# Short-conv rows behind the last input slab, fewer products per LayerNorm statistic, and two swish buffers

## The reference

```python
z = h @ w_in                                   # 7 groups of 1024 columns
b_a, c_a, x_a, u_b, v_b, g_a, g_b = jnp.split(z, cuts, axis=-1)
y_a = (b_a * depthwise_conv(c_a * x_a, conv_a)) @ w_a_out      # 3 taps
u = u_b * jax.nn.sigmoid(v_b)
u = depthwise_conv(u, conv_b) + b_conv_b                       # 31 taps
u = jax.nn.silu(layernorm(u, ln_g, ln_b))                      # over the 1024 channels
y_b = u @ w_b_out
m = jax.nn.sigmoid(g_a) * y_a + jax.nn.sigmoid(g_b) * y_b
return m @ w_o
```

## Time and profile before

| | |
|---|---|
| time, median of 3 runs | 1763.46 us (1763.32 to 1764.2) |
| the profiled execution's own time | 1762.71 us |
| its span, first to last instruction | 1760.9 us |
| mean granted TensorE clock | 0.961 of full speed |
| busy: PE, VectorE (DVE), ACT, GpSimd (POOL) | 1587.8, 1336.4, 682.0, 339.0 us |

### The profile page before, as it was taken

One profiled execution on the slowest core, in us unless ns is written; L12 is line 12 of the kernel. 1 busy time (PEld: TensorE's weight loads), 2 busy tenths in 40 slices (PEclk: granted clock), 3 DMA queues, 4 the chain that ended last, 5 costly groups with the idle time before them and its releaser, 6 DMA issues.

```text
span 1760.9 us, 21630 instructions
## 1 busy us (share of the span) xinstructions
PE 1587.8 (90%) x7040; PEld 1290.2 (73%) x7040; DVE 1336.4 (76%) x1152; ACT 682.0 (39%) x574; POOL 339.0 (19%) x208
## 2 busy tenths in 40 slices
PE   2799999999999997997989965999999999999981
PEld 2688888888888885775777854788887777777861
DVE  5687869678696878349435446999999999899984
ACT  4401121121111202214213122777776766676762
POOL 1100000000000000000000002255454444345440
PEclk9999999999999998998999975999999999999995
DMA  7413323142232315423426253999999999999945
GB/s 267 142 54 115 107 94 108 60 131 83 84 107 95 107 48 194 128 72 120 132 85 201 101 203 124 348 366 371 373 360 361 361 351 358 359 352 356 370 143 208
DMA packets 167572, 352.07 MB, mean 200 GB/s; under 512 B 17229, under 2 KB 90957, under 8 KB 167542
## 3 DMA queue, kind: packets, MB, share of 16 engines
q1 hardware_dynamic: 150838, 309.71, 49.9%
q0 software_dynamic: 16704, 41.98, 7.9%
HBM read 323.84 MB, written 46.66 MB: 210 GB/s over the span
## 4 chain that ended last, share of the span: by engine, by line
PE 59%; DMA 18%; DVE 13%; issue 4%; ACT 4%; POOL 1%; DVEq 0%; SPq 0%; POOLq 0%; ACTq 0%
PE ps L1220 18%; PE ps L1222 18%; PE ps L1221 18%; DMA e_raw<-in_w_down_dram 15%; DVE e_lo L1148 3%; ACT e_hi L723 2%; DMA xg<-d_h,g_idx 2%; DVE e_lo L1144 2%; PE ps L1276 2%; DVE macc L836 1%; PE ps L1394 1%; PE ps L1342 1%; DVE s L951 1%; DVE conf L942 1%; DVE f_o L1210 1%
## 5 line engine op out<-in xcount | busy, mean ns | idle before, releaser
L1220 PE MATMUL ps<-A_hi,w_hi 128*128 128x512 f32 x1024 | 402.9, 393 | 23.8 <-DVE A_lo L931 13.0
L1221 PE MATMUL ps<-A_lo,w_hi 128*128 128x512 f32 x1024 | 401.0, 392 | 0.0
L1222 PE MATMUL ps<-A_hi,w_lo 128*128 128x512 f32 x1024 | 400.9, 392 | 0.0
L1144 DVE TENSOR_TENSOR e_lo<-e_raw,e_hi 128x2048 fp32r<-128x2048 f32 x136 | 309.0, 2285 | 12.4 <-ACT e_hi L717 10.8
L921 DVE SCALAR_TENSOR_TENSOR conv_acc_b<-glu,colc,conv_acc_b 128x1024 f32<-128x1024 f32 x232 | 298.0, 1285 | 10.4 <-DVE rows L913 0.3
L717 ACT CAST e_hi<-e_raw 128x2048 fp32r<-128x2048 f32 x136 | 259.7, 1912 | 61.3 <-PE ps L1222 56.1
L1220 PEld LDWEIGHTS ps<-A_hi,w_hi 128*128 128x128 f32 x1024 | 194.0, 189 | 66.9 <-issue 17.8
L1221 PEld LDWEIGHTS ps<-A_lo,w_hi 128*128 128x128 f32 x1024 | 194.1, 190 | 40.7 <-issue 0.5
L1222 PEld LDWEIGHTS ps<-A_hi,w_lo 128*128 128x128 f32 x1024 | 193.8, 189 | 40.6
L1220 PE MATMUL ps<-e_hi,xT_hi 128*128 128x512 f32 x528 | 212.6, 403 | 0.0
L1222 PE MATMUL ps<-e_hi,xT_lo 128*128 128x512 f32 x528 | 206.9, 392 | 0.0
(11 more groups left out here) (227 smaller groups left out, 2025.5 us busy)
## 6 DMA issues: line engine op xcount, KB each, us to landing
e_raw<-in_w_gate_dram SPq DMA_DIRECT2D x132, 512.0 KB, 5.5
e_raw<-in_w_up_dram SPq DMA_DIRECT2D x132, 512.0 KB, 12.4
e_raw<-in_w_down_dram SPq DMA_DIRECT2D x66, 1024.0 KB, 14.0
w_raw<-in_w_in_dram SPq DMA_DIRECT2D x56, 512.0 KB, 4.3
stream<-in_w_ada_dram SPq DMA_DIRECT2D x48, 512.0 KB, 5.7
xn<-in_x_dram SPq DMA_DIRECT2D x8, 512.0 KB, 7.0
d_short<-conv_acc_a POOLq DMA_DIRECT2D x8, 512.0 KB, 4.0
d_gate_a<-gate_st POOLq DMA_DIRECT2D x8, 512.0 KB, 2.9
```

Of the source, the lines that this page charges most:

```text
L1144: v.tensor_tensor(e_lo[:, q, :], e_raw[:, q, :], e_hi[:, q, :].bitcast(F32), ALU.subtract).then_inc(gu_lo, 1)
L1220: t.matmul(dst, st_hi, mv_hi, start=first, stop=False)
L1221: t.matmul(dst, st_hi, mv_lo, start=False, stop=False)
L1222: return t.matmul(dst, st_lo, mv_hi, start=False, stop=last)
```

## The change

- *Rows of the short conv.* The last of the 8 channels is unrolled on PE, VectorE, ACT and GpSimd. In its last slab PE signals every finished k (`s_lastk`), and ACT overwrites `A_hi[k]` at once, ahead of the evacuation of gate B. VectorE has no taps in kinds 4 and 5 and all of taps 15 to 30 in kind 6, behind the eight `A_lo` and a weight split. PE no longer waits for gate B's evacuation before slab 0.
- *Sums.* GpSimd adds the conf tiles 0 to 6 up in the last tile's place (one add in each of the first 7 channels) and copies the sum to `conf_sum`; the mean takes `conf_sum` and the last tile. VectorE adds the squares up in two sums of four (`add_squares`, 6 adds among the centrings), and the variance takes those two. It moves from behind slab 4 into slab 3, between its sixth and seventh k.
- *Root, LayerNorm, swish.* The root moves from j = 4 to j = 3, with two fused instructions in place of three. LayerNorm's scale and shift go from VectorE to ACT (an Identity). Sigmoids and products alternate between two buffers each, `B_lo` of a tile comes after the product of the next, and tiles go by 2, 3 and 3 in j = 4, 5 and 6.

```diff
+            pool.wait_ge(s_xT, NT)
+            running = conf[:, (KT - 1) * S:KT * S]
+            g.memset(running, 0.0).then_inc(s_csum, 1)
+            with pool.Fori(0, KT - 1) as ch:
+                channel(ch)
+                held(s_conf, ch + 1)
+                pool.wait_ge(s_csum, ch + 1)
+                g.tensor_tensor(running, running, conf[:, bass.ds(ch * S, S)], ALU.add).then_inc(s_csum, 1)
+            pool.wait_ge(dve_evac, (KT - 1) * 3 + 1 + CREDIT_DVE_EVAC)
+            pool.wait_ge(s_csum, KT)
+            g.tensor_copy(conf_sum[:], running).then_inc(s_csum, 1)
+            channel(KT - 1)
...
+                    if last and kind == NK - 1:           # ACT
+                        for k in range(KT):
+                            wait_tile(act, M_A + k)
+                            if k < KT - 1:
+                                act.wait_ge(s_lastk, k + 1)
+                            else:
+                                act.wait_ge(pe_slab, n_done)
+                            a.copy(A_hi[:, k, :], tile(M_A + k)).then_inc(s_ahi, 1)
...
-                for k in {4: [0, 1], 5: [2, 3], 6: [4, 5], 7: [6, 7]}.get(j, []):
+                for k in LN_STEPS.get(j, []):              # {4: [0, 1], 5: [2, 3, 4], 6: [5, 6, 7]}
                     swish_in(k)
-                    conf_hi(k)
+                    if k >= 1:
+                        conf_hi(k - 1)
...
+            LAST_TAPS = {1: range(0, 5), 2: range(5, 11), 3: range(11, 15), 6: range(15, KB)}
...
+                    if last and kind == NK - 1:           # VectorE
+                        for k in range(KT):
+                            dve.wait_ge(s_ahi, k + 1)
+                            v.tensor_tensor(A_lo[:, k, :], tile(M_A + k), A_hi[:, k, :].bitcast(F32), ALU.subtract).then_inc(s_alo, 1)
+                            dve.wait_ge(s_alo, k + 1)
+                            dve.sem_inc(st_free[(M_A + k) % 4], 1)
+                        split(W_SLOT[k2], ch * NK + (kind + 3))
...
+                dve.wait_ge(s_lsig, 2 * k + 2)
+                if k >= 2:
+                    dve.wait_ge(s_blo, k - 1)
+                v.tensor_tensor((s2 if k % 2 else ln_sw0)[:], conf[:, k * S:(k + 1) * S], (ln_sig1 if k % 2 else s1)[:],
+                                ALU.mult).then_inc(s_sw, 1)
                 if k >= 1:
+                    conf_lo(k - 1)
+                if k + 2 < KT:
+                    ln_t(k + 2)
...
+                        if k == 3:
+                            add_squares(0, 1, 2, 0)
+                        if k == 5:
+                            add_squares(2, 3, 4, 0)
+                    add_squares(0, 2, 4, 2)
+                    add_squares(4, 5, 6, 0)
+                    add_squares(6, 7, 8, 0)
+                    add_squares(4, 6, 8, 5)
...
-                    step(v.tensor_tensor(s2[:], s2[:], ps[:, 3, :], ALU.mult))
-                    step(v.tensor_scalar(s2[:], s2[:], -0.5, 1.5, ALU.mult, ALU.add))
-                    step(v.tensor_tensor(ps[:, 3, :], s1[:], s2[:], ALU.mult))
+                    step(v.scalar_tensor_tensor(s2[:], s2[:], -0.5, ps[:, 3, :], ALU.mult, ALU.mult))
+                    step(v.scalar_tensor_tensor(ps[:, 3, :], s2[:], 1.5, s1[:], ALU.add, ALU.mult))
...
+            def mean():
+                pe.wait_ge(act_evac, CREDIT_ACT_EVAC + 4 * KT)
+                pe.wait_ge(s_csum, KT + 1)
+                pe.wait_ge(s_conf, KT)
+                statistic(ps[:, 2, :], [conf_sum[:], conf[:, (KT - 1) * S:KT * S]], s_mean)
+            def variance():
+                pe.wait_ge(s_sqs, 6)
+                statistic(ps[:, 3, :], [conf_sq[:, 0, :], conf_sq[:, 4, :]], s_var)
```

More of the change, by code:

```diff
@@ L634, in _ @@
                           ch * NK + (kind + 2 - W_BACK[k2] + 1 + CREDIT_SLAB))
+            with act.Fori(0, KT - 1) as ch:
+                channel(ch, False)
+            channel(KT - 1, True)
             n0 = NK * KT
[L637 to L640, removed]
             def split2(n):
@@ L647, in swish_in @@
             def swish_in(k):
+                u = conf[:, k * S:(k + 1) * S]
+                g_col, b_col = cols[:, k, ROW_LN_G:ROW_LN_G + 1], cols[:, k, ROW_LN_B:ROW_LN_B + 1]
                 act.wait_ge(s_ln, k + 1)
[L649 to L652, removed]
+                if k >= 2:
+                    act.wait_ge(s_sw, k - 1)
+                a.activation((ln_sig1 if k % 2 else s1)[:], u, ACT.Sigmoid, scale=g_col, bias=b_col).then_inc(s_lsig, 1)
+                act.wait_ge(s_lsig, 2 * k + 1)
+                a.activation(u, u, ACT.Identity, scale=g_col, bias=b_col).then_inc(s_lsig, 1)
             def conf_hi(k):
                 act.wait_ge(s_sw, k + 1)
-                a.copy(B_hi[:, k, :], s2[:]).then_inc(s_bhi, 1)
+                a.copy(B_hi[:, k, :], (s2 if k % 2 else ln_sw0)[:]).then_inc(s_bhi, 1)
             for j in range(KT):
@@ L908, in _ @@
                     k2 = (kind + 2) % NK
-                    split(W_SLOT[k2], ch * NK + (kind + 3))
+                    if not (last and kind == NK - 1):
+                        split(W_SLOT[k2], ch * NK + (kind + 3))
                     if kind in (0, 2, 4, 6):
@@ L915, in _ @@
                         dve.sem_inc(st_free[q], 1)
-                    for t in TAPS.get(kind, []):
+                    if last and kind == NK - 1:
[4 more added lines that the diff above has]
+                            dve.sem_inc(st_free[(M_A + k) % 4], 1)
+                        split(W_SLOT[k2], ch * NK + (kind + 3))
+                    for t in (LAST_TAPS if last else TAPS).get(kind, []):
                         w = colc[:, t:t + 1]
@@ L926, in _ @@
                 assert count[0] == N_STEPS, count
+            with dve.Fori(0, KT - 1) as ch:
+                channel(ch, False)
+            channel(KT - 1, True)
             n0 = NK * KT
[L929 to L933, removed]
             def split2(n):
@@ L1261, in _, with channel @@
                 6: (act_evac, 4, CREDIT_ACT_EVAC + 2)}
-            with pe.Fori(0, KT) as ch:
+            def channel(ch, last):
                 for kind in range(NK):
@@ L1266, in _, with statistic @@
                     pe.wait_ge(w_lo_done, ch * NK + (kind + 1 + CREDIT_SLAB))
-                    slab_product(W_SLOT[kind], ps[:, PS_SLOT[kind], :], s_hlo if kind == 0 else None).then_inc(pe_slab, 1)
+                    slab_product(W_SLOT[kind], ps[:, PS_SLOT[kind], :], s_hlo if kind == 0 else None,
+                                 s_lastk if last and kind == NK - 1 else None).then_inc(pe_slab, 1)
+            with pe.Fori(0, KT - 1) as ch:
+                channel(ch, False)
+            channel(KT - 1, True)
             n0 = NK * KT
-            def statistic(dst, src, ready, done):
-                for k in range(KT):
-                    pe.wait_ge(ready, k + 1)
+            def statistic(dst, parts, done):
+                for n, part in enumerate(parts):
                     for h in range(2):
-                        last = t.matmul(dst[:, h * H:(h + 1) * H], mean_w[:], src(k, h), start=(k == 0), stop=(k == KT - 1))
+                        last = t.matmul(dst[:, h * H:(h + 1) * H], mean_w[:], part[:, h * H:(h + 1) * H],
+                                        start=(n == 0), stop=(n == len(parts) - 1))
                 last.then_inc(done, 1)
-            pe.wait_ge(act_evac, CREDIT_ACT_EVAC + 4 * KT)
+            def mean():
[6 more added lines that the diff above has]
+                statistic(ps[:, 3, :], [conf_sq[:, 0, :], conf_sq[:, 4, :]], s_var)
             pe.wait_ge(dve_evac, CREDIT_DVE_EVAC + 3 * KT)
```

53 lines of the change are left out of this document (34 added, 19 removed).

## The result

The changed kernel takes 1722.06 us (median of 4 runs, 1719.55 to 1723.56), the kernel before, in the runs taken with it, 1763.83. The ratio is 0.9762, 95% interval 0.9749 to 0.9774: 2.4% faster, 41.8 us. The forecast was 1721, 42.4 us less.

What follows compares the result with a forecast made beforehand. PE, busy 90% of the span, was taken as the bound. Statistics 20.6, swish waits 16.7 and rows 16.2 - 8.3 - 2.8 = 5.1 made 42.4 us less: 1721 expected, range 1712 to 1730.

Steps and rivals of the forecast that it cites:

- The first wait: After the last w_in slab, before slab 0: PE's 13.0 us without work was to disappear.
- T: Time when the last channel's conf is complete and the mean can start: forecast 708.4, bounds 703.3 and 710.5.
- stretch: From the last w_in slab's end to the first w_b_out slab's end: 158.26 us before, forecast 115.9.
- Clock: At the mean, after PE idles 8.3 us: 5.5 us at half pace lose 2.75, so the mean takes 6.2 us.
- S: End of slab 3 with the variance, from which VectorE starts evacuation, split and root; forecast 31.4 us after conf is complete.
- waits of 16.7 us: Swish part: PE's waits for a w_lo (5.6 us) and B_lo (6.2 us) and slowness after them were to go.
- Margin: Before the first w_b_out slab's last B_lo: ready 2.0 us before PE asks for it, so hidden.
- rival 2: Swish loop keeps its old 4.4 us a channel: 6.8 us later, 1727.8; chance 0.24 together with the loop-exit rival.
- rival 4: GpSimd adds hold VectorE every channel; slower than before only above 12.6 us per add; chance 0.03 with all else.
- rival 1: Tiles or clock kinder: conf complete at 703.3, clock stays up through 3.2 us idle, 1713.2 us; chance 0.14.
- 3: PE's loop exit at 602 us stalls up to 5.07 us: up to 1726.1; chance 0.24 together with the swish-pace rival.
- 5: Two together: taps end 8 us later and the swish part loses its 6.8, 1735.8 us; chance 0.07.

Runs made afterwards that it cites:

- the second profile: Changed kernel, unedited, profiled again on the same chip; its span from the last w_in slab to the first w_b_out slab took 114.52 us.
- u_rows: Changed kernel with the short conv's rows back at their old place, last channel still unrolled; 1724.0 us, ratio 0.9782.
- f_taps8: Changed kernel with taps 15 to 19 back in kind 4 and three more among the A_lo; 1712.06 us, ratio 0.9708.
- u_sums: Changed kernel with both statistics over eight tiles again, no adds on GpSimd or VectorE; 1742.38 us, ratio 0.9877.
- f_warm: Changed kernel with nine extra discarded float32 matmuls on PE between slab 1 and the mean; 1720.86 us, ratio 0.9755.
- u_swish: Changed kernel with the old swish body: single buffers, LayerNorm's scale on VectorE, B_lo behind its own product; 1729.57 us, ratio 0.9810.
- u_root: Changed kernel with variance and root one slab later, LayerNorm tiles two each in j = 4 to 7; 1727.39 us, ratio 0.9805.
- g_x9: Changed kernel with nine GpSimd instructions of 128x1024 per channel in place of one; 1760.41 us, ratio 0.9981.
- f_taps5: Changed kernel with taps 15 to 19 of the last channel back in kind 4; 1714.51 us, ratio 0.9721.

## Why the prediction was right

- *The first wait goes, a wait for the taps comes.* Right in place and size: 13.0 us gone, 8.3 us at the mean (forecast 8.33). T came out 0.2 us from the forecast: the last tile was taken by ACT 9.8 us after the first A_lo, where 10.0 were taken over from the old train, and T repeats within 0.5 us in the second profile. u_rows bears out the net worth, 5.04 for 5.1 us, within the 2 us to which a stretch repeats, and f_taps8 the reason: with the taps out of the way the same reorder gives 15.75.
- *Statistics.* 20.6 us forecast, 20.09 shown by u_sums. The step that carried it was to count records: 16 matmuls are 32 records, so a product of two tiles has 8.
- *Clock.* Forecast loss 2.75 us; the mean lost 2.5 (5.94 for 3.43), and f_warm gives back 2.3 of it.
- *Centring, adds and variance.* Hidden, as forecast: S = T + 31.4.
- *Root and swish.* The waits of 16.7 us are gone. Margin 2.0 us forecast, 2.9 in the trace. u_swish shows that the new swish body (buffers, scale on ACT and order together) is worth 6.8, the place of the root 6.2 (u_root). That rival 2 had 6.8 as its price too is chance: it left out the clock, which makes 1.3 of the measured one, and had the margin at 2.0. These overlap within the 16.7 us and don't add up by themselves; the way from the old to the new swish part, with both undone, wasn't tried.
- *GpSimd.* Price 0 for one add, right, with the hold coming out of idle time. What the add holds at the head of the channel shown is the 128x41 copy, and not the w_lo split or the rows step that the prediction named. The threshold of rival 4 came out about right: in the channel shown for g_x9 the rows of VectorE from the split at 648.67 to the one at 676.35 are together some 14 us longer than their like in the kernel before, and the kernel is back at its old time; the forecast had 12.6 us. The add itself takes 2.40 us, where the nearest row had 1.88. Where it would bite was wrong: not before glu but behind it.
- *Loop exit on PE.* No wait near 602 us: price 0.
- *Rivals.* 1, 2, 3 and 5 did not happen. What rival 1 priced (T earlier and no slow clock, 1713.2) is near what f_taps5 reached by another way (1714.5).
- *What was luck.* The stretch came out within 0.3 us of the forecast, while two executions of the same kernel differ by 1.15. So the mechanism and the terms were right, but the last digit of the sum could not be. The late start, 1.97 us, wasn't in the forecast of the profiled execution either: 1720.3 against 1722.2.

What the forecast missed costs nothing in its number, but was there to be read: when the taps of kinds 4 and 5 are moved, VectorE idles 7.4 us ahead of them.

## What to carry to other kernels

When work is moved behind something urgent on an engine, lay out that engine's timeline for the new order and look for the hole it leaves: here 5 of 11 moved taps fit into the hole, and they were worth 9 us of the stretch, 6.9 of the wait that had only changed its place and the rest its clock. Price such a move by the next consumer of everything queued behind it; the first wait's length is only an upper bound. Here the sums over partitions on TensorE cost by the record, so adding tiles up beforehand on engines with idle time paid in full, as long as what GpSimd takes from VectorE stays inside VectorE's idle time.

## What the runs showed of the hardware

- A VectorE copy of 128x41 lasted 2.42 us beside a GpSimd add of 128x1024, 0.19 without. Two-operand VectorE instructions are held too: four taps 13.32 us instead of 5.25 beside a row of GpSimd adds, which themselves went from 2.41 to 3.16 us. A product with one operand in PSUM took 1.23 us beside such an add, as alone.
- The clock's fall doesn't go by the length of one wait: after 1.9 us of waiting for w_lo in u_swish PE had a granted clock of 0.70 in the next 5.7 us, while in u_root a wait of 3.1 us and in f_taps5 one of 1.5 left it at 1.00:

```profile
776.00:780.00 4.00, 3.85 (x17) 3.20 (x18) 4.00 (x5) 3.97 (x5) 0.00 (x0) 1.00 0.98 294
```

(u_root, directly behind its wait.) In g_x9 the clock was 1.00 from 205 to 211, behind a wait of 3.56 us, and 0.50 from 532 to 534, behind one of 3.54. Nor is its return the same each time: 0.59 or 0.77 in the same 6 us of two executions of one kernel.
